# Second key step of two branches: one transpose on 32 partitions, two rounded copies and two rests per half, in a two-group decoder step

## What is computed

```
def trunk(x, states, p):
    for l in range(DEPTH):
        x = swiglu_half(x, p['ffn1_norm'][l], p['ffn1_w_up'][l], p['ffn1_w_down'][l])
        y, st = mixer(rmsnorm(x, p['mix_norm'][l]), l, lb_all[l], p, tuple(s[l] for s in states))
        x = x + y
        x = swiglu_half(x, p['ffn2_norm'][l], p['ffn2_w_up'][l], p['ffn2_w_down'][l])

def gated_linear_scan(q, k, v, logf, s0):      # HGRN2 (branch 0), GLA (branch 1)
    """S_t = diag(exp(logf_t)) S_{t-1} + k_t v_t^T ; o_t = S_t^T q_t"""
    def step(s, inp):
        ...
        s_new = (jnp.exp(b_end[:, :, 0, :])[..., None] * s
                 + jnp.einsum('bhsd,bhsv->bhdv', kc * jnp.exp(b_end - b), vc))
```

## Time and profile before

| | |
|---|---|
| median of 3 runs | 2896.9 us (2896.18 to 2897.35) |
| the profiled execution | 2895.75 us |
| its span, first to last instruction | 2894.0 us |
| TensorE busy | 2860.7 us (99%) |
| GpSimd busy | 1585.0 us (55%) |
| VectorE busy | 1669.0 us (58%) |
| ScalarE busy | 946.0 us (33%) |
| mean granted TensorE clock | 0.997 |

### The profile page before, as it was taken

One profiled execution on the slowest core, in us unless ns is written; L12 is line 12 of the kernel. 1 busy time (PEld: TensorE's weight loads), 2 busy tenths in 40 slices (PEclk: granted clock), 3 DMA queues, 4 the chain that ended last, 5 costly groups with the idle time before them and its releaser, 6 DMA issues.

```text
span 2894.0 us, 60445 instructions
## 1 busy us (share of the span) xinstructions
PE 2860.7 (99%) x23436; PEld 2810.0 (97%) x23436; DVE 1669.0 (58%) x2419; ACT 946.0 (33%) x1604; POOL 1585.0 (55%) x1466
## 2 busy tenths in 40 slices
PE   8999999999999999999999999999999999999998
PEld 7999999999999999999999999999999999999998
DVE  8663676544453568373784737755444436783745
ACT  4221233022142425251452514320412423452433
POOL 6666776555554674525454253755565556734343
PEclk9999999999999999999999999999999999999999
DMA  5796836565655654353344433364665556443532
GB/s 188 201 254 193 215 102 195 151 157 140 172 156 127 179 166 154 120 174 111 126 142 132 163 111 110 122 179 143 168 162 144 158 150 177 161 151 121 164 119 80
DMA packets 196945, 444.10 MB, mean 153 GB/s; under 512 B 13464, under 2 KB 57664, under 8 KB 195904
## 3 DMA queue, kind: packets, MB, share of 16 engines
q1 hardware_dynamic: 107360, 281.09, 29.7%
q0 software_dynamic: 40128, 125.83, 18.3%
q10 hardware_dynamic: 49248, 34.28, 4.0%
HBM read 422.64 MB, written 144.35 MB: 196 GB/s over the span
## 4 chain that ended last, share of the span: by engine, by line
PE 93%; DVE 3%; POOL 1%; issue 1%; ACT 1%; DMA 1%; DVEq 0%; ACTq 0%; PEld 0%; POOLq 0%; SPq 0%
PE dense L713 60%; PE SA L773 14%; PE SB L773 10%; PE SA L916 1%; PE SA L902 1%; POOL Wl L579 1%; PE SA L843 1%; PE SA L988 1%; PE SA L991 1%; PE SA L887 0%; PE SA L830 0%; POOL Wh L577 0%; PE SB L995 0%; DMA pair<-w_sums 0%; PE SB L839 0%
## 5 line engine op out<-in xcount | busy, mean ns | idle before, releaser
L579 POOL TENSOR_TENSOR Wl<-raw,Wh 128x512 fp32r<-128x512 f32 x620 | 849.0, 1369 | 51.8
L577 POOL TENSOR_SCALAR Wh<-raw 128x512 fp32r<-128x512 f32 x620 | 444.5, 717 | 725.6 <-PEq L718 484.4
L713 PE MATMUL dense<-Hh,Wh 128*128 128x272 f32 x2784 | 588.2, 292 | 12.4 <-POOLq L581 10.4
L713 PE MATMUL dense<-Hh,Wl 128*128 128x272 f32 x2784 | 576.7, 289 | 0.0
L713 PE MATMUL dense<-Hl,Wh 128*128 128x272 f32 x2784 | 575.2, 288 | 0.0
L713 PEld LDWEIGHTS dense<-Hh,Wh 128*128 128x128 f32 x2784 | 436.9, 189 | 24.1 <-issue 17.4
L713 PEld LDWEIGHTS dense<-Hl,Wh 128*128 128x128 f32 x2784 | 438.3, 189 | 0.0
L713 PEld LDWEIGHTS dense<-Hh,Wl 128*128 128x128 f32 x2784 | 435.8, 189 | 0.0
L642 POOL TENSOR_TENSOR Sl<-pair,Sh 128x512 fp32r<-128x512 f32 x120 | 172.4, 1454 | 430.1 <-ACT Sh L1078 429.2
L713 PE MATMUL dense<-Ah,Wh 128*128 128x272 f32 x1408 | 291.9, 289 | 0.8 <-DVE X L1794 0.7
L713 PE MATMUL dense<-Al,Wh 128*128 128x272 f32 x1408 | 290.7, 288 | 0.0
(11 more groups left out here) (468 smaller groups left out, 6357.7 us busy)
## 6 DMA issues: line engine op xcount, KB each, us to landing
raw<-wst SPq DMA_DIRECT2D x276, 512.0 KB, 3.6
w_sums<-wst POOLq DMA_DIRECT2D x36, 1536.0 KB, 13.3
w_sums<-wst POOLq DMA_DIRECT2D x18, 2048.0 KB, 16.2
pair<-wst SPq DMA_DIRECT2D x120, 256.0 KB, 3.5
pair<-w_sums SPq DMA_DIRECT2D x60, 512.0 KB, 3.7
wsum<-w_sums SPq DMA_DIRECT2D x60, 512.0 KB, 3.6
w_sums<-w_sums POOLq DMA_DIRECT2D x12, 1536.0 KB, 8.2
wsum<-wst SPq DMA_DIRECT2D x60, 256.0 KB, 2.5
```

The lines of the kernel that those rows point to most:

```text
L577: pool.tensor_scalar(Wh[:, j, cs], raw[:, j, cs], 1.0, 0.0, ALU.mult, ALU.add).then_inc(glink, 1)
L579: pool.tensor_tensor(Wl[:, j, cs], raw[:, j, cs], f32(Wh[:, j, cs]), ALU.subtract).then_inc(glink, 1)
L713: mm = pe.matmul(dps[slot][:, a, 0:HALF], w[:, ring, w0:w0 + 128], x[:, k, a * HALF:(a + 1) * HALF], start=(k == 0 and n == 0), stop=(k == ...
```

## The change

In k 1 of branches 0 and 1, TensorE turns the sample rows once, to partitions 0 to 31 of `SA`, and no longer to the other three groups. ScalarE reads these 32 partitions twice for each half e and writes the rounded copies to groups 0 and 1 of `kst`; VectorE reads them twice for each half and writes the rests to groups 2 and 3, taking the rounded copy of group 0 as what it subtracts. Branch 2 stays as it was. The count of `k_hi` per layer goes from 12 to 16. `HALVES_BEHIND` is unchanged.

```diff
@@ -936,8 +936,10 @@
+                        elif br == 2:
+                            four(SA[:, 0, i * P:(i + 1) * P], K[:, i, SEQ:TOK], ident)
                         else:
-                            four(SA[:, 0, i * P:(i + 1) * P], K[:, i, SEQ:TOK], ident)
+                            tpose(SA[0:SMP, 0, i * P:(i + 1) * P], K[:, i, SEQ:TOK], ident)
@@ -1352,9 +1354,9 @@
-                            if br < 2:
-                                act.activation(kst[:, e, 0:nt, :].rearrange("p a b -> p (a b)"),
-                                               SA[:, 0, 0:nt * P], ACT.Copy, scale=half_of[:, e:e + 1]).then_inc(k_hi, 1)
+                            for g in (slice(0, SMP), slice(SMP, 2 * SMP)) if br < 2 else ():
+                                act.activation(kst[g, e, 0:nt, :].rearrange("p a b -> p (a b)"), SA[0:SMP, 0, 0:nt * P],
+                                               ACT.Copy, scale=half_of[0:SMP, e:e + 1]).then_inc(k_hi, 1)
@@ -2032,14 +2034,15 @@
-                        dve.wait_ge(k_hi, L * 12 + (2, 4, 12)[br])
+                        dve.wait_ge(k_hi, L * 16 + (4, 8, 16)[br])
                     for e in range(2 * h):
...
-                        if br < 2:
-                            x = kst[lo, e, 0:nt, :].rearrange("p a b -> p (a b)")
-                            ch.did(STT(x, SA[lo, 0, 0:nt * P], half_of[lo, e:e + 1], f32(x), ALU.mult, ALU.subtract))
+                        for g in (slice(2 * SMP, 3 * SMP), slice(3 * SMP, P)) if br < 2 else ():
+                            ch.did(STT(kst[g, e, 0:nt, :].rearrange("p a b -> p (a b)"), SA[0:SMP, 0, 0:nt * P],
+                                       half_of[0:SMP, e:e + 1],
+                                       f32(kst[0:SMP, e, 0:nt, :].rearrange("p a b -> p (a b)")), ALU.mult, ALU.subtract))
```

## The result

The changed kernel takes 2906.28 us in the median of 9 runs (2905.58 to 2907.99), the kernel before 2897.35 in 9 runs beside it (2895.53 to 2901.26). The ratio is 1.0029, 95% interval 1.0020 to 1.0038: slower by 8.9 us, 0.3%, clear of noise and outside the range of the prediction. The profiled execution of the changed kernel took 2907.26 us, with a span of 2905.5.

A forecast was written before the change was run, and what follows sets the result against it. TensorE, holding 93% of the chain, was taken as the bound. Its savings of 1.55 and 0.64 us per layer, outweighed by stalls behind k 1, summed to +2.8 on 2896.9, giving 2899.7 us, range 2896.0 to 2903.0.

The forecast's parts named there:

- The direction of the sum: k 1, both branches: stalls outweigh TensorE's saving, +1.2 us in branch 0 and +0.2 in branch 1, +2.8 over two layers.
- the mechanism of the cover: Behind k 1: ScalarE's and VectorE's work is free only while the half tile, about 3.2 us, covers it.
- TensorE saves 1.55 and 0.64: k 1 of branches 0 and 1: the step shortens from 2.92 to 1.37 us and from 1.79 to 1.15.
- the bound of 0.8 for drained transposes: k 1: if each 32-column transpose took 0.21 us instead of 0.11, 0.8 us is lost over two layers; chance 0.07.
- The cover is all but used up in branch 0: Behind k 1: u starts no more than 0.21 us behind VectorE's end already; forecast new stall 2.7 us, branch 1 0.8.
- What ScalarE now takes: Behind k 1: four copies for two, 2.39 us in branch 0 (1.12 more), 1.55 in branch 1 (0.71 more).
- the other row, that of v: VectorE's rests behind k 1: no overlap when groups alternate, so four take 3.09 us in branch 0, 2.05 in branch 1.
- The hop: From VectorE's last rest to TensorE's start of u: between 0.13 and 0.21 us, taken as 0.17.
- The stall costs TensorE its clock: Rival, dense work and u behind branch 0's stall: half clock adds 3.4 to 6.8 us, giving 2903.1 to 2906.5; chance 0.08.
- The rival's own price: Behind branch 0's stall: a half-clock stretch of 3.50 us costs 1.7 us, one of 7.20 us costs 3.4.
- The chances: Whole kernel, threshold 0.2%: the same 0.92, slower 0.07, faster 0.01.

The follow-up runs named there:

- the order by group: Changed kernel with ScalarE's copies and VectorE's rests reordered so each engine finishes one partition group before the next; 2901.80 us against 2897.96 before.
- the wait filled: Changed kernel with twelve idle identity products ahead of u in branch 0; 2903.36 us against 2898.24 before.
- with wide un: Changed kernel with step un's one-column matmuls made 128 columns wide and its four-column ones moved behind them; 2899.45 us, ratio to before 1.0005.
- the copies alone: Changed kernel with TensorE again writing all four groups in k 1, keeping the four copies and four rests; 2909.57 us against 2898.24 before.
- TensorE's part alone: Kernel before with only the single transpose per tile in k 1 of branches 0 and 1, copies and rests unchanged; 2895.03 us against 2898.24.
- the restored cover: Changed kernel with one more half tile behind k 1 and one less behind u, branches 0 and 1; 2895.36 us against 2898.24 before.
- the early start: Order by group, plus ScalarE making group 1 from group 0 in SBUF and VectorE waiting for two copies; 2897.10 us against 2897.96 before.
- the wide kernel before: Kernel before with un's one-column matmuls made 128 columns wide and its four-column ones moved behind them; 2891.61 us against 2897.91.

## Why the prediction was wrong

The direction of the sum and the mechanism of the cover held. The step that failed is the one that left TensorE's clock at its full level behind the new stall: it stood in the sum at nothing, and its rival had a chance of 0.08. The lost clock measures some 4.4 us, about 2.8 of it from the stall. A second term, ScalarE's copies, was too small by 1.6 us over four steps.

- **TensorE saves 1.55 and 0.64**: measured 1.58 and 0.67. Four transposes on 32 columns run at 0.11 each, like wide ones; the bound of 0.8 for drained transposes fell.
- **The cover is all but used up in branch 0**: held, and it decided. The new wait is 3.05 us where I had 2.7, and 1.1 where I had 0.8.
- **What ScalarE now takes** was mis-sized: 2.80 us for 2.39, and 1.94 for 1.55. I took the overlapped pace of before for copies that alternate between two groups. For VectorE I had picked the other row, that of v, and 3.07 for 3.09 shows it right. The Trainium skill's rule (VectorE: DVE Perf Modes, "Two Vector instructions with no wait between them") holds with 0.77 for 0.74 per rest, and the order by group confirms it; that ScalarE shows the same no row had told me, and I did not carry it over. This is 0.4 us per step, and 1.6 over four steps.
- **The hop** of 0.17 was 0.19. The waits less the savings come to 4.2 where I had 2.8; the difference is ScalarE's, less 0.03 more saved on TensorE in each step.
- **The stall costs TensorE its clock** was the rival that came true. I gave it 0.08, because ahead of the first norm TensorE stood idle for 2.3 us and the clock was 1.00 behind it. That was one execution. Behind the wait at that place the clock fell in five of the fourteen profiles, the changed kernel's own among them. Over 17 runs the changed kernel lost 4.4 us more to the clock than before, and with the wait filled 2.8 to 2.9 us of its loss went away. The rival's own price, 1.7 for a stretch, was right (1.63). That its result, 2903.1 to 2906.5, holds the 2906.28 measured is part luck: it had the waits at 2.8 where they cost 4.2, and its upper end took twice the half clock behind each stall that any profile shows. The waits alone, 2896.9 + 4.2 = 2901.1, would have stayed in the range 2896.0 to 2903.0; the clock took the time out of it.
- **The chances** followed from that: 0.92 for no change rested on one profile's row being a rule. The range allowed un 1.7 us either way, from a profile in which un had less half clock than in any other.

What stays open: how often the clock falls behind a wait of a given length. Of eight waits of 3.05 us in four profiles (the changed kernel twice, with wide un, and with the copies alone) four had half clock behind them, while the 2.8 us that filling won is the price of 1.7 stretches per execution; behind the waits of 2.5 us (by group) none of two in the profile, but 0.9950 in the mean of the runs suggests that some do; behind those of 1.1 to 1.3 us none in any profile. I have not varied the length alone. Some 1 to 1.6 of the 4.4 us of lost clock is not assigned to a place; by one profile each it may be un's, which no experiment shows. The medians of TensorE's part alone, of the restored cover and of the early start gain about 1 us less than the lag says (3.2 for 4.5, 2.9 for 4.2, 0.9 for 1.7), which is inside their intervals and was not followed up.

## What to carry to other kernels

Where a scan step is covered by work of TensorE, write down the whole chain that runs under that cover, its semaphore hops too, before shortening TensorE's part: here 3.2 us of cover stood over 2.9 and a hop of 0.2. TensorE's saving showed when that chain stayed as it was, and again when the cover grew with the longer chain, and not in between. Splitting one instruction over 128 partitions into several over 32 costs each its full length, and if they alternate between groups of partitions, their overlap as well; order them by the group written. And price a new wait of TensorE of a few us with the clock that may follow it, from several executions: one profile in which it stayed up says little, while the mean granted clock over the runs, times the span, gives what is lost.

## What the hardware showed that I had not expected

- ScalarE too overlaps two instructions only if they write to the same group of 32 partitions: starts 0.57 us apart (1.25 for two of 0.68), and 0.71 if the group changes.
- A wait of 3.05 us was followed by some 3.4 us at half clock in four of eight cases, at about 1.6 us each, one of 2.4 us in three of twelve, and one of 3.3 us in both. Filling the waits of 3.05 us with useless matmuls kept the clock behind all four of them that were profiled, and took nothing from the path.
- The width of un's matmuls costs nothing. In the chain of the wide kernel before, the step takes 3.57 + 1.68 = 5.25 us in layer 0 (rows below). In the kernel before, a head at full clock takes 0.89 + 0.45, so four take 5.3 to 5.4. The edit won 6.3 us over both layers: in all four profiles with it the clock stays at its full level in un, where in the ten without it it fell for 3.4 to 10.2 us per layer. All those matmuls had one or four columns; since the order changed too, the width is the likely cause and not shown by itself.

The chain of one head of un in layer 0 in the kernel before, then that of the whole wide step:

```profile
916.46 0.89 PE SA L957 x8
917.35 0.45 PE SA L961 x4
```

```profile
914.72 3.57 PE SA L957 x32
918.29 1.68 PE SA L962 x16
```
